# A four-stack transformer step on one core: the split weights' buffers start 32 bytes later in their partition

## The reference, cut to what matters

```python
def _swiglu(h, w_in, w_out):
    g, u = jnp.split(h @ w_in, 2, axis=-1)
    return (jax.nn.silu(g) * u) @ w_out
...
        h = h + gm * (mix_l @ mix_w_out[layer])
```

## Time and profile before

| | |
|---|---|
| median of three runs | 3036.04 us |
| lowest, highest | 3035.89, 3038.37 us |
| profiled execution, its span | 3035.4 us |
| TensorE matmul busy | 2979.4 us, 98% |
| weight loads busy | 2629.2 us, 87% |
| VectorE busy | 1691.5 us, 56% |
| ScalarE busy | 1314.2 us, 43% |
| matmuls | 20172 |
| mean granted TensorE clock | 0.996 of 2.4 GHz |
| moved by DMA | 439.36 MB, mean 145 GB/s |

### The profile page before, as it was taken

The page is one execution under the profiler, slowest core; times in us unless marked ns, Lnnn a source line. Parts: engine busy times, 40 slices in busy tenths (PEclk is TensorE's granted clock), DMA queues, the critical chain, the costliest instruction groups (busy, mean ns, idle before and its releaser), DMA issues.

```text
span 3035.4 us, 52037 instructions
## 1 busy us (share of the span) xinstructions
PE 2979.4 (98%) x20172; PEld 2629.2 (87%) x20172; DVE 1691.5 (56%) x2664; ACT 1314.2 (43%) x1952; POOL 0.2 (0%) x4
## 2 busy tenths in 40 slices
PE   8999999999999999999999999999999999999999
PEld 6778878787777878888889999999899999998998
DVE  4333363544332453334666667677766676787666
ACT  4322333423222332223345555555654554556544
POOL 0000000000000000000000000000000000000000
PEclk9999999999999999999999999999999999999999
DMA  9564342055576433333324655455456645554564
GB/s 276 174 185 133 115 146 82 30 167 167 172 212 184 132 100 88 110 90 92 110 71 117 188 167 158 144 155 166 133 159 181 180 124 163 155 155 142 155 183 129
DMA packets 639011, 439.36 MB, mean 145 GB/s; under 512 B 22172, under 2 KB 627192, under 8 KB 638712
## 3 DMA queue, kind: packets, MB, share of 16 engines
q1 hardware_dynamic: 637844, 436.70, 48.3%
q10 hardware_dynamic: 996, 0.23, 0.0%
HBM read 430.84 MB, written 1.05 MB: 142 GB/s over the span
## 4 chain that ended last, share of the span: by engine, by line
PE 88%; DVE 7%; ACT 2%; issue 1%; SPq 1%; DMA 1%; DVEq 0%; ACTq 0%
PE ps L453 27%; PE ps L455 26%; PE ps L454 26%; PE ps L541 2%; DVE wlo L402 2%; ACT whi L396 1%; PE ps L1803 1%; PE ps L1771 1%; DMA raw<-ffn_w_in 1%; DVE normed L2666 1%; PE ps L1791 1%; SPq L717 1%; DVE xl L2658 0%; PE ps L1252 0%; PE ps L1261 0%
## 5 line engine op out<-in xcount | busy, mean ns | idle before, releaser
L453 PE MATMUL ps<-xh,whi 128*128 128x256 f32 (+1 forms) x3744 | 1218.3, 325 | 23.1 <-DVE wlo L402 5.1
L454 PE MATMUL ps<-xl,whi 128*128 128x256 f32 (+1 forms) x3744 | 1197.2, 320 | 0.0
L455 PE MATMUL ps<-xh,wlo 128*128 128x256 f32 (+1 forms) x3744 | 1197.1, 320 | 0.0
L402 DVE TENSOR_TENSOR wlo<-raw,whi 128x1024 fp32r<-128x1024 f32 x732 | 868.9, 1221 | 186.9 <-ACT whi L396 178.2
L396 ACT ACTIVATE whi<-raw 128x1024 fp32r<-128x1024 f32 x731 | 746.5, 1052 | 472.2 <-PE ps L455 412.6
L453 PEld LDWEIGHTS ps<-xh,whi 128*128 128x128 f32 x3744 | 713.8, 191 | 105.3 <-issue 43.4
L455 PEld LDWEIGHTS ps<-xh,wlo 128*128 128x128 f32 x3744 | 714.0, 191 | 50.8
L454 PEld LDWEIGHTS ps<-xl,whi 128*128 128x128 f32 x3744 | 714.7, 191 | 48.8
L453 PE MATMUL ps<-hid_h,whi 128*128 128x512 f32 (+1 forms) x1056 | 355.9, 337 | 0.0
L454 PE MATMUL ps<-hid_l,whi 128*128 128x512 f32 (+1 forms) x1056 | 354.9, 336 | 0.0
L455 PE MATMUL ps<-hid_h,wlo 128*128 128x512 f32 (+1 forms) x1056 | 354.8, 336 | 0.0
(11 more groups left out here) (380 smaller groups left out, 2595.4 us busy)
## 6 DMA issues: line engine op xcount, KB each, us to landing
raw<-ffn_w_in SPq DMA_DIRECT2D x176, 512.0 KB, 4.6
mod_w<-ada_w SPq DMA_DIRECT2D x72, 1024.0 KB, 7.5
raw<-w_in SPq DMA_DIRECT2D x96, 512.0 KB, 4.5
raw<-w_ffn_in SPq DMA_DIRECT2D x88, 512.0 KB, 4.7
raw<-w_gate SPq DMA_DIRECT2D x64, 512.0 KB, 4.0
raw<-ffn_w_out SPq DMA_DIRECT2D x64, 384.0 KB, 4.0
raw<-ffn_w_out SPq DMA_DIRECT2D x64, 320.0 KB, 3.6
raw<-w_branch SPq DMA_DIRECT2D x32, 512.0 KB, 3.4
```

Source lines behind the costliest of these rows:

```text
L402: nc.vector.tensor_tensor(wlo[:, s, h, :], raw[:, s, h, :], whi[:, s, h, :].bitcast(F32), ALU.subtract).then_inc(S("lo_ready"), 1)
L453: nc.tensor.matmul(dst, w_h, x_h, start=start, stop=False)
L454: nc.tensor.matmul(dst, w_h, x_l, start=False, stop=False)
L455: return nc.tensor.matmul(dst, w_l, x_h, start=False, stop=stop)
```

## The change

`whi` begins 32 bytes later, and with it `wlo`, which follows it. Another 32 bytes are left free behind `wlo`, so that `hT` and all that lies behind it moves by 64 bytes. `raw` and all in front of it stays.

```diff
         raw = fixed("raw", [P, 2, 2, UNIT // 2])
+        fixed.at += 32
         whi = fixed("whi", [P, 2, 2, UNIT // 2], F32R)
         wlo = fixed("wlo", [P, 2, 2, UNIT // 2], F32R)
+        fixed.at += 32
         hT = fixed("hT", [P, DC, 2 * T])
```

## The result

The kernel with the change takes 3042.57 us in the median of 16 runs (3040.33 to 3046.25); the kernel before, run beside it, 3037.01 us (16 runs, 3035.56 to 3039.09). The ratio is 1.0018, with a 95% interval of 1.0011 to 1.0025: slower by 0.18%, where 1.2% faster had been forecast. It lies within the 0.2% that the prediction set as "no change", but outside its range. All lines of the kernel are two further down: L455 to L457 are L453 to L455 of before, L398 is L396, L404 is L402.

A forecast was written before the change was run, and what follows sets the result against it. The prediction took the pace at which TensorE's matmuls start behind each other as the bound. Its terms, (25.3 + 14.5 - 1.9) x 0.95 = 36.0 us, off 3036.04 gave 3000.0 us, range 2975 to 3040 us.

The forecast's parts named there:

- What the bound is: Whole kernel: TensorE is busy 98% of the span, so the pace at which matmuls start behind each other makes the time.
- each gains 2.5 ns: Matmuls of `x` and `hid` at 256 wide: each of 10128 gains 2.5 ns, 25.3 us in all.
- the swapped form: 384 x 3 of the 256-wide matmuls, counted in the 25.3 us gain; both operands were said to get the new relation.
- I take 2.67 ns, since the equal 13.3 ns says that the rest is of one kind: 512-wide matmuls: both widths carry 13.3 ns beside their columns, so each of 5424 saves 2.67 ns, 14.5 us.
- the weight load was at 188 ns at 512 wide already: Evidence against a 512-wide gain: weight loads take 192 ns with `x` at 256 wide, but 188 ns at 512.
- slower: the pace at 512 wide comes loose: Rival, 512-wide matmuls: starts wander, 25 us on top; 3061 us, or 3039 with the 256-wide gain; chance 0.14.
- Its price of 4.6 ns, from the small weights: Loss per 512-wide matmul, from the first mixer's small weights, whose starts lie 231.3 ns apart against 226.7.
- its point of decision: Loss from which slower decides: 4.1 ns per 512-wide matmul if 256-wide ones gain, any loss if they do not.
- they lose the relation: Matmuls streaming `h_y`: both operands are then 32 bytes off, so 768 x 2.5 ns, 1.9 us, is given back.
- The twentieth taken off: Whole sum times 0.95, because the first few matmuls behind each break and at stage changes have gaps of their own.
- The split: L396 on ScalarE and L402 on VectorE: at most 11 and 5 ns either way, beside TensorE, costing nothing.
- The page against it: Skill rules on TensorE's waits and weight loading: pace independent of the stationary operand's place, sum 0 against 36 us.

The follow-up runs named there:

- x32: Kernel before with `xh`, `xl`, `hid_h`, `hid_l` 32 bytes past a multiple of 64, `h_yh`, `h_yl` at one, weights left: 3050.68 us, ratio 1.0044.

## Why the prediction was wrong, and where it was right

**What the bound is: right.** The time is the pace of the matmuls; no wait, queue or other engine moved it. The chain keeps its shares and the ledger of matmul distances accounts for the whole 6.7 us between the two traces.

**256 wide, "each gains 2.5 ns": right in size, with a wrong reason behind it.** `x` and `hid` gained 2.51 ns each, 22.6 us on 8976 of the 10128; the swapped form, counted in with them, gained only 1.2 ns, and there the streamed operand is the weights and d is 224. But the change did not give `x` the relation of `h_y`. That was 160 by 256 and `x` got 32; that its 117.4 ns lies close to the 116.7 and 117.8 that `x` then had was luck.

**512 wide, "I take 2.67 ns, since the equal 13.3 ns says that the rest is of one kind": this is the step that failed.** In its place the runs show a loss: 226.7 became 233.3 ns, 5.7 ns on the average of the ledger, +30.9 us where -14.5 was taken (about 6.2 ns and 34 us without the two stretches at the lower clock in the trace of before). The equal 13.3 ns at both widths was no sign of one mechanism with one remedy: d = 0 (120.0 ns) is with d = 96 the slowest placing of the table at 256 wide, and the fastest at 512. In every other placing in the table 512 wide pays from 2.2 to 7.6 ns more, so among the placings tried there was nothing to gain there. With +30.9 put for -14.5, and the other terms as taken, the sum would have been some 7 us slower instead of 36 faster. The misreading had a warning that the prediction named and set aside: the weight load was at 188 ns at 512 wide already.

**The rival that came true.** It is "slower: the pace at 512 wide comes loose", in its form with a gain at 256 wide: 3039 us forecast, 3042.6 measured. Its price of 4.6 ns, from the small weights, was 1.1 ns short of 5.7 (1.6 short of 6.2), and its point of decision, 4.1 ns for each 512-wide matmul, was passed. The case was given 0.14, and against it stood that "the small weights fill 32 columns of the array". The relation offers another reading: the chunks of `e_small_h` are 128 bytes apart, so their d alternates between 0 and 128, whose paces in the table are 226.7 and about 233. Their mean is about 230, where the earlier trace rows shows 231.3, so the reading is argued and not shown; whether the columns play a part was not tried.

**`h_y`, "they lose the relation": wrong in sign.** 1.9 us back was forecast, 1.2 us were gained. d went from 160 to 192, whose better pace is 113.3 ns. Where `h_y` did get the relation 0 that the prediction had in mind, in `x32`, it lost its pace as forecast and ran at 120.0.

**The twentieth taken off** stands for the runs' beginnings; in the ledger the average at 256 wide is the full 2.5 ns, so it was not needed.

**The split: right.** 1221 ns on VectorE as before, 4 ns more on ScalarE, both beside the matmuls.

**The page against it.** The rule of the Trainium skill (SBUF — State Buffer, section on two separate sides) that TensorE never waits on anyone would, as the prediction applied it, have given no change, and the total came close to that, but as the difference of two terms of 31 and 23 us, neither of which the rule allows. The Trainium skill's page TensorE: Matmul & The Clock Gate (step by step) has the streamed and the stationary operand on two read ports that take nothing from each other. The measured paces, 113.3 to 120.2 ns for one shape by the relation of the two starts, speak against that as far as time goes. What inside the chip makes them depend on each other no run here shows.

## What to carry to other kernels

Where float32r matmuls follow each other with a weight load each, read the pace of each width and operand from the starts in the timeline, and write down the start of the streamed operand less that of the stationary one, by 256 bytes: in steps of 32 bytes that relation moved the pace by 6% at 256 wide and by 3% at 512. Do not carry a gain from one width to the other, even where both show the same excess over their columns; here the placing that is best at 512 wide, d = 0, is among the slowest at 256. Place the buffers by stage, where stages differ in width (1.2% here), and measure the placing in the kernel itself, since an isolated loop can settle at another pace.

## What the runs showed of the hardware that was not expected

- The pace of triples goes by the relation of the two starts with a period of 256 bytes: from 113.3 to 120.2 ns at 256 wide and from 226.7 to 234.3 at 512 in steps of 32. Moving both starts together left 120.0 and 226.7 ns at all seven placings tried.
- One placing can hold two steady paces (117.8 and 113.3 ns at d = 192), and what ran before picks one: the starts 32 and 96 settled at 117.8 behind fp32 matmuls and at 113.3 behind every other stretch tried.
- Relations below 32 bytes count too, and among them are the slowest of all: at 256 wide 4 bytes gave 123.4 ns, 8 bytes 126.7 and 16 bytes 116.8; at 512 wide 237.8, 233.3 and 231.4.
- A pace seen in isolation need not come in the kernel: 112 bytes gave 113.3 ns alone and 120.0 in the kernel. This is open.
